# Low parts of two activation sums moved from VectorE to GpSimd in four feed-forward stages of a float32 decoder step

## What is computed

```python
def ffn_half(h, g_pre, g_post, w_in, w_out):
    a = rmsnorm(h, g_pre) @ w_in            # 576 x 1024 @ 1024 x 5632
    gate, up = jnp.split(a, 2, axis=-1)
    return h + FFN_RESID * rmsnorm((jax.nn.silu(gate) * up) @ w_out, g_post)
```

## Time and profile before

| | |
|---|---|
| median of three runs | 2304.41 us (2304.14 to 2310.2) |
| the profiled execution's own time | 2308.2 us |
| its span, first to last instruction | 2306.5 us |
| TensorE busy | 2250.6 us |
| VectorE, ScalarE, GpSimd busy | 1384.5, 1022.2, 457.7 us |
| granted TensorE clock, mean | 0.994 |

### The profile page before, as it was taken

The page is one execution under the profiler, slowest core; times in us unless marked ns, Lnnn a source line. Parts: engine busy times, 40 slices in busy tenths (PEclk is TensorE's granted clock), DMA queues, the critical chain, the costliest instruction groups (busy, mean ns, idle before and its releaser), DMA issues.

```text
span 2306.5 us, 38990 instructions
## 1 busy us (share of the span) xinstructions
PE 2250.6 (98%) x14416; PEld 2031.3 (88%) x14416; DVE 1384.5 (60%) x2815; ACT 1022.2 (44%) x2156; POOL 457.7 (20%) x296
## 2 busy tenths in 40 slices
PE   8999999999899999999999999999999999999998
PEld 7999988986556899998889999888999779999887
DVE  6999700587431699980069998005576648999402
ACT  5655422534322655551255555125332446555322
POOL 1000134250312200004310000432254220000332
PEclk9999999999998999999999999999999999999999
DMA  3233422232671322334232323322212323322422
GB/s 116 92 101 97 138 84 81 73 114 81 210 250 55 119 78 92 100 97 131 82 118 79 102 95 108 122 83 86 65 56 60 148 86 122 99 92 97 142 82 87
DMA packets 101450, 237.60 MB, mean 103 GB/s; under 512 B 12396, under 2 KB 29293, under 8 KB 101006
## 3 DMA queue, kind: packets, MB, share of 16 engines
q1 hardware_dynamic: 98190, 224.62, 30.4%
q0 software_dynamic: 3072, 10.49, 1.4%
HBM read 220.17 MB, written 14.89 MB: 102 GB/s over the span
## 4 chain that ended last, share of the span: by engine, by line
PE 85%; DVE 6%; ACT 3%; DMA 2%; issue 2%; POOL 0%; SPq 0%; DVEq 0%; ACTq 0%; POOLq 0%
PE psum L2396 33%; PE psum L2334 7%; PE psum L2336 7%; PE psum L2335 7%; PE psum L2200 5%; PE psum L2202 5%; PE psum L2201 5%; PE psum L2327 2%; PE psum L2328 2%; PE psum L2763 1%; PE psum L2618 1%; PE psum L2681 1%; DMA a_r<-ffn_in 1%; ACT y L814 1%; DVE y L1456 1%
## 5 line engine op out<-in xcount | busy, mean ns | idle before, releaser
L1308 POOL TENSOR_TENSOR w_lo<-raw,w_hi 128x1024 fp32r<-128x1024 f32 (+1 forms) x157 | 373.2, 2383 | 1636.3 <-ACT w_hi L800 1636.2
L800 ACT ACTIVATE w_hi<-raw 128x1024 fp32r<-128x1024 f32 (+1 forms) x171 | 178.9, 1048 | 453.3 <-DMA raw<-ffn_out 344.5
L1456 DVE TENSOR_TENSOR y<-psum,g_post 128x512 f32<-128x512 f32 x48 | 32.4, 689 | 547.1 <-ACT y L814 546.5
L2334 PE MATMUL psum<-w_hi,gu 128*128 128x512 f32 x704 | 275.3, 391 | 3.5 <-issue 2.6
L2335 PE MATMUL psum<-w_hi,gu 128*128 128x512 f32 x704 | 274.1, 389 | 0.0
L2336 PE MATMUL psum<-w_lo,gu 128*128 128x512 f32 x704 | 274.0, 389 | 0.0
L2396 PE MATMUL psum<-t_lo,s_hi_r 128*128 128x288 f32 x928 | 273.3, 294 | 0.0
L2200 PE MATMUL psum<-x_hi,w_hi 128*128 128x320 f32 (+1 forms) x880 | 266.3, 303 | 0.3
L2201 PE MATMUL psum<-x_lo,w_hi 128*128 128x320 f32 (+1 forms) x880 | 261.5, 297 | 0.0
L2202 PE MATMUL psum<-x_hi,w_lo 128*128 128x320 f32 (+1 forms) x880 | 261.4, 297 | 0.0
L912 ACT ACTIVATE s_hi_r<-s_r 128x512 fp32r<-128x512 f32 x304 | 189.1, 630 | 121.6 <-DVE s_r L1620 120.9
(11 more groups left out here) (342 smaller groups left out, 5331.4 us busy)
## 6 DMA issues: line engine op xcount, KB each, us to landing
a_r<-ffn_in SPq DMA_DIRECT2D x280, 256.0 KB, 2.8
raw<-ffn_out SPq DMA_DIRECT2D x88, 512.0 KB, 3.6
raw<-gla_in SPq DMA_DIRECT2D x25, 512.0 KB, 3.7
raw<-ffn_in SPq DMA_DIRECT2D x24, 512.0 KB, 4.3
cache<-cache POOLq DMA_DIRECT2D x64, 160.0 KB, 3.3
cache<-cache SPq DMA_DIRECT2D x64, 160.0 KB, 3.5
c_k<-cache_kt SPq DMA_DIRECT2D x64, 128.0 KB, 2.9
a_x<-ffn_in SPq DMA_DIRECT2D x24, 256.0 KB, 2.9
```

Source lines behind the costliest of these rows:

```text
L800: act.activation(w_hi[slot][:, 0:w], raw[slot][:, 0:w], ACT.Copy).then_inc(s_hi, 1)
L1308: pool.tensor_tensor(w_lo[slot][:, 0:w], raw[slot][:, 0:w], w_hi[slot][:, 0:w].bitcast(F32), ALU.subtract).then_inc(s_lo, 1)
L1456: dve.tensor_tensor(dst, y_bank(b, t, half), post_gain(t, half), ALU.mult).then_inc(s_evicted, 1)
L2334: pe.matmul(dst, w[0], m[0], start=start, stop=False)
```

## The change

In each feed-forward GpSimd makes the low parts of sums 1 and 2, before it waits for the plain blocks; the two calls on VectorE are gone. The counts of the semaphores stay the same: GpSimd waits for the high part and for the low part before.

```diff
@@ GpSimd
             def ffn(st):
+                f = ffn_no[st]
+                for i, order in ((1, 3), (2, 4)):
+                    pool.wait_ge(f_thi, 4 * f + order)
+                    pool.wait_ge(f_x, N_FX * f + 7 + order)
+                    pool.tensor_tensor(t_lo[i][:, :, :], t_f[i][:, :, :], t_hi[i].bitcast(F32), ALU.subtract).then_inc(f_x, 1)
                 pool.wait_ge(s_lo, first_block[st] + FB)
                 out_phase(st, 0)
@@ VectorE, group(g)
                     low_form("s3", g, 4 if g > 0 else 5, 3)
                     if g > 0:
                         low_part(g - 1, c_1[(g - 1) % 2], 2 * a, 0)
-                    if g == 0:
-                        x_low_form(1, 3)
                     if more:
                         sum_1(g + 1)
@@ VectorE, group(g)
                     if more:
                         part_low("a11", g + 1, 1, 1)
-                    if g == 0:
-                        x_low_form(2, 4)
                     dve.wait_ge(f_e, 3 * a + 2)
```

## The result

The changed kernel takes 2314.67 us (median of 18 runs, 2310.22 to 2319.99), against 2306.70 us for the kernel before in the same comparison (18 runs, 2301.97 to 2313.16). The ratio is 1.0036, with an interval of 1.0028 to 1.0044: 8.3 us slower, between 6.5 and 10.1. The forecast was 2309.5 us with a range to 2313.5, so the sign and the two holds come out as forecast; the order of service at the second hold does not, and the size lies outside. The profiled execution took 2313.33 us in its own time.

What follows compares the result with a forecast made beforehand. TensorE was taken to bound the kernel, with VectorE setting its stalls where groups begin. Four feed-forwards at 1.27 us gave +5.1 us on a median of 2304.4, so 2309.5 us, range 2306.5 to 2313.5.

Steps and rivals of the forecast that it cites:

- the two holds: In each feed-forward, GpSimd's two operations each block a VectorE operation with two SBUF operands until they end.
- What bounds: TensorE, busy 2250.6 of 2306.5 us; its late starts, set by VectorE where groups begin, total 8.7 us, all the possible gain.
- what is removed: Two VectorE operations in each feed-forward, 1.27 us each, 10.2 us of VectorE's time over four.
- what is added: Eight operations on GpSimd, taken as 2.70 us each, bounds 2.41 and 3.18.
- long-operation rival: GpSimd's operation takes 2.94 us or more, making the kernel slower beyond 0.3%; 2313.3 us at 3.18; chance 0.13.
- What it does to VectorE: The deciding term: VectorE operations with two SBUF operands wait until GpSimd's operation ends; those with one in PSUM pass.
- not held: Rival: GpSimd doesn't block VectorE, which is 2 x 1.27 us earlier in each feed-forward; 8.3 us less, 2296.1; chance 0.05.
- First hold: At VectorE's low part of gate times up: s4 x b22 starts 1.43 us late, VectorE itself only 0.42.
- Second hold: At VectorE's low part of a22: a22 x t_4 starts 1.27 us late, and both engines stay that late.
- Who comes next?: GpSimd, asking at about 67.55, is let in behind two back-to-back VectorE operations, at 68.27, after a11's low part.
- the rival: GpSimd goes first, behind VectorE's running operation; a11's low part is stretched; +1.65 us each feed-forward, 2311.0 in all; chance 0.22.
- Afterwards: Behind the held a22, both engines stay 1.27 us late, group 1's stalls stay, and nothing gives the time back.

Runs made afterwards that it cites:

- e5: Changed kernel, but GpSimd's second operation also waits until VectorE has made the low part of the next group's a11: 2313.59 us, one run.
- e4: Changed kernel with GpSimd's two subtractions replaced by memsets to zero, leaving out the low parts of sums 1 and 2: 2300.25 us, ratio 0.9966.
- e2: Changed kernel with only sum 1's low part on GpSimd, sum 2's again on VectorE: 2310.21 us, ratio 1.0008 against the kernel before.
- e9: Whole computation left out: six back-to-back VectorE subtractions of 512 columns, GpSimd's request moved ever later; GpSimd's operation took 1.27 us at 0.07 ahead, 1.82 at 0.02.
- e10: As e9, with VectorE at 576 columns and GpSimd at 256, on 64 then 128 partitions: GpSimd took 0.72 to 0.91 us, the last request 1.36.
- e12: As e9, with rounded outputs; the second twelve trials put a 64x320 subtraction and 128x128 copy ahead of the chain: GpSimd there took 3.33 to 3.69 us.
- e1: The changed kernel again, no edit: 2315.44 us against 2308.76 for the kernel before, ratio 1.0030.

## Why the prediction was right or wrong

- **What bounds, what is removed, what is added: right.** TensorE keeps the end. GpSimd's operation takes 2.76 and 2.79 us with a short wait in it; in e5, where VectorE's running operation read PSUM when GpSimd asked, it took 2.67 to 2.68, for the 2.70 taken. The long-operation rival is out.
- **What it does to VectorE: right.** Both holds are there (2.51 and 3.16 us), and e4 shows what they cost: some 15 us between the subtraction and the memset on GpSimd. The forecast for "not held" was 8.3 us faster; e4 measured 7.8.
- **First hold: right to 0.01 us.** s4 x b22 is 1.42 us late for 1.43; e2 leaves 0.4 us in a feed-forward for the 0.42 of VectorE's lateness.
- **Second hold, "Who comes next?": wrong.** I took the one attention row, by which GpSimd waits for two back-to-back operations. It was served behind the running one, and a11's low part was stretched, which the text had named as the sign of the rival. The rival's own working holds: TensorE's product at 70.97 on the old scale, measured 71.95 - 1.01 = 70.94; price 1.65 us, measured 1.61 (79.77 - 78.16). The Trainium skill, cited there from "SBUF — State Buffer" (section "SBUF: two separate sides"), gives the pair to whichever engine starts first, for its whole instruction; read as the rival reads it, that gave the same, and e9, e10 and the first half of e12 agree but for requests under about 0.03 us ahead. The second half of e12 and the place at 1671 us don't: there GpSimd waits through the chain. I had read the two operations that met and not what stood right ahead of them. Nor was the row "the only such place of the trace": the one at 1671 us is a second, and it too speaks for late service, so what was missing was the condition, not the case. The error is worth 4 x (1.61 - 1.27) = 1.4 us.
- **Afterwards: wrong in two points.** Nothing gave the lateness back, as forecast. But the stalls of group 1 didn't stay: the first is gone and the second is 0.59 us for 0.82, as the rival had it (e5, with the forecast's order, keeps both). And the sum has no term for the places outside the groups where the two engines meet. The third hold, at 508 us, costs 1.4 us once.
- **The centre: 2.3 us from the sample.** The median of three runs before was 2304.4; eighteen gave 2306.7. The runs of one kernel spread by 10 to 11 us, and most of that goes with the granted clock: of e1's 29 runs of the kernel before, the three at a mean of 0.998 took 2302.5 to 2304.2 us, the five at 0.993 took 2309.1 to 2311.8. So a range of 7 us about a median of three was narrow, whatever the mechanism.
- **The sum again.** From the forecast of 2309.5 to the measured 2314.67 are 5.2 us: 2.3 of the sample, 1.4 of the order of service and 1.4 of the third hold. With the larger sample, 2306.7 + 4 x 1.61 + 1.4 = 2314.5 us. One or two of the three would have left the time inside the range; it took all of them. That the sum closes to 0.2 us is partly luck: the ratio's interval is 6.5 to 10.1 us, and e1 gave 6.9.

## What to carry to other kernels

Moving a two-operand elementwise operation from VectorE to GpSimd frees VectorE of its own step (here 1.27 us) and, wherever VectorE reads two operands from SBUF, holds it for most of GpSimd's length (here 2.1 and 2.5 us of 2.7); going by these runs it helps only where VectorE would be idle, reading PSUM, or where GpSimd doesn't read SBUF. When a forecast rests on one row that disagrees with a simple rule, read what stands ahead of that row on both engines, and search the trace for every other place of its kind. After a change, compare the stretches that it didn't touch product by product: 0.15 us can decide which of two engines goes first somewhere else. And before giving an engine a lead, look for its next wait on another engine: the lead ends there unless that wait moves too.

## What the runs showed that was not expected

- Behind a copy within SBUF at the head of a chain (with the 64x320 subtraction ahead of it), VectorE isn't interrupted through five back-to-back operations, and a GpSimd operation of 0.72 us takes 3.33 to 3.69 us (e12). Late service without a copy stands at 1671 us of the kernel before (3.21 us for 2.41).
- In the chains of equal two-operand operations (e9, e10, the first half of e12) a request of GpSimd is served at the end of VectorE's running operation if it comes some 0.05 us or more before the next would start, and one operation later if it comes 0.02 us before (0.72 against 1.35 us in e12, 1.27 against 1.82 in e9).
- A GpSimd memset of 128x1152 takes 1.07 us and holds no operation of VectorE (e4).
- The order of service flipped at one place that no edit touched, some 445 us after the first changed operation, and cost 1.4 us: VectorE 0.12 us ahead of GpSimd before, 0.03 us behind it now.
